# Decoded tokens' states and head norms as pieces of the streamed work of a hybrid decoder's mixers, and streamed work between dependent steps of VectorE

## The reference

```python
def _mixer(x, st, p, l):
    u = x @ p['w_in'][l] + p['b_in'][l]        # one projection for all branches and gates
    o_a, ... = _rwkv7(rw, ...)                  # RW: generalized delta rule, head norm
    o_b, ... = _mlstm(mqk, mv, mo, mi, mf, ...) # ML: matrix memory, causal conv, head norm
    o_c, ... = _gla(gq, gk, gv, gg, ga, ...)    # GL: gated linear attention, head rms
    o_d, ... = _rglru(rx, ry, ...)              # RG: gates, causal conv, linear scan
    up = einsum('blgc,gcd->blgd', branches, p['w_branch'][l])
    gate = sigmoid(gates.reshape(B, L, 4, 1024))
    return einsum('blgd,blgd->bld', gate, up) @ p['w_out'][l], new_states
```

## Time and profile before

| | us |
|---|---|
| median of 3 runs | 1965.49 |
| lowest, highest | 1957.01, 1965.77 |
| the profiled execution | 1960.32 |
| its span | 1958.5 |
| PE busy | 1805.5 (92%) |
| DVE busy | 1383.6 (71%) |
| ACT busy | 939.5 (48%) |

### The profile page before, as it was taken

The page is one execution under the profiler, slowest core; times in us unless marked ns, Lnnn a source line. Parts: engine busy times, 40 slices in busy tenths (PEclk is TensorE's granted clock), DMA queues, the critical chain, the costliest instruction groups (busy, mean ns, idle before and its releaser), DMA issues.

```text
span 1958.5 us, 26391 instructions
## 1 busy us (share of the span) xinstructions
PE 1805.5 (92%) x10174; PEld 1527.9 (78%) x10174; DVE 1383.6 (71%) x1619; ACT 939.5 (48%) x968; POOL 15.2 (1%) x32
## 2 busy tenths in 40 slices
PE   8799989979998989989986999999899999999896
PEld 7678878879997868868865877777687877777685
DVE  4857864445652758885425988989797979888794
ACT  4323422243332524422214666666576657766673
POOL 1000000000001000000000000000000000000000
PEclk9789999999998979999995999999999999999999
DMA  6233322334552324321223988989798978989770
GB/s 244 94 107 141 123 87 72 124 151 173 186 182 77 130 87 159 127 97 65 109 105 155 343 320 298 346 305 340 272 347 306 340 282 323 346 320 344 278 299 23
DMA packets 59307, 402.81 MB, mean 206 GB/s; under 512 B 8672, under 2 KB 9344, under 8 KB 11312
## 3 DMA queue, kind: packets, MB, share of 16 engines
q1 hardware_dynamic: 54144, 393.73, 54.0%
q0 software_dynamic: 1600, 3.97, 0.6%
q10 hardware_dynamic: 3440, 3.41, 0.5%
HBM read 396.60 MB, written 4.49 MB: 205 GB/s over the span
## 4 chain that ended last, share of the span: by engine, by line
PE 81%; DVE 11%; ACT 4%; issue 3%; DMA 0%; ACTq 0%; DVEq 0%; SPq 0%
PE mA L1906 48%; PE mW L1906 31%; ACT WH L703 2%; DVE slots_rounded L1270 1%; PE mA L1837 1%; DVE SCR L1235 1%; ACT X L994 1%; DVE SCR L1352 0%; DMA slots<-in_w_in_dram 0%; DVE V L1709 0%; DVE SCR L1347 0%; PE mW L1909 0%; DVE BIG L1285 0%; DVE HEL L1172 0%; DVE SCR L1237 0%
## 5 line engine op out<-in xcount | busy, mean ns | idle before, releaser
L1050 DVE TENSOR_TENSOR ring_low<-ring,WH 128x2048 fp32r<-128x2048 f32 x216 | 493.0, 2289 | 92.6 <-ACT WH L703 92.0
L703 ACT ACTIVATE WH<-ring 128x2048 fp32r<-128x2048 f32 x212 | 405.0, 1913 | 79.6 <-PE mW L1906 64.4
L1906 PE MATMUL mA<-XH,slots_rounded 128*128 128x264 f32 x1696 | 378.3, 297 | 10.2 <-DVE slots_rounded L1270 9.2
L1906 PE MATMUL mA<-WH,XEH 128*128 128x512 f32 x704 | 293.9, 418 | 8.2 <-DVE XEL L1140 6.9
L1906 PEld LDWEIGHTS mA<-XH,slots_rounded 128*128 128x128 f32 x1696 | 286.5, 194 | 17.8 <-issue 12.7
L1906 PE MATMUL mA<-WH,XEL 128*128 128x512 f32 x704 | 277.0, 393 | 0.0
L1906 PE MATMUL mA<-ring_low,XEH 128*128 128x512 f32 x608 | 240.2, 395 | 0.0
L1906 PE MATMUL mA<-XL,slots_rounded 128*128 128x264 f32 x672 | 197.2, 293 | 6.5 <-DVE small L1549 5.6
L1906 PEld LDWEIGHTS mA<-WH,XEH 128*128 128x128 f32 x704 | 133.1, 189 | 39.3 <-DVE ring_low L1050 10.6
L1906 PEld LDWEIGHTS mA<-WH,XEL 128*128 128x128 f32 x704 | 132.9, 189 | 31.9
L1906 PEld LDWEIGHTS mA<-XL,slots_rounded 128*128 128x128 f32 x672 | 130.3, 194 | 11.4 <-DVE small L1549 7.3
(11 more groups left out here) (396 smaller groups left out, 3135.7 us busy)
## 6 DMA issues: line engine op xcount, KB each, us to landing
ring<-in_moe_dram SPq DMA_DIRECT2D x216, 1024.0 KB, 4.8
slots<-in_w_in_dram SPq DMA_DIRECT2D x58, 1024.0 KB, 4.8
more_ring<-in_moe_dram SPq DMA_DIRECT2D x48, 1024.0 KB, 4.8
slots<-in_ffn_up_dram SPq DMA_DIRECT2D x22, 1024.0 KB, 4.8
slots<-in_ffn_down_dram SPq DMA_DIRECT2D x12, 1024.0 KB, 4.8
slots<-in_w_branch_dram SPq DMA_DIRECT2D x8, 1024.0 KB, 4.7
slots<-in_w_out_dram SPq DMA_DIRECT2D x8, 1024.0 KB, 4.8
con<-in_const_dram SPq DMA_DIRECT2D x1, 1441.0 KB, 14.4
```

Source lines behind the costliest of these rows:

```text
L703: nact.activation(WH[:, HI_SLOT[j % PAIR], :], expert_slot(j), ACT.Copy).then_inc(weights_hi, 1)
L1050: v.tensor_tensor(expert_low(j), expert_slot(j), WH[:, HI_SLOT[j % PAIR], :].bitcast(F32), SUB)\
L1906: return nc.tensor.matmul(out, w, x, start=start, stop=stop, skip_group_check=True)
```

## The change

It does five things in both mixers.

1. The decoded tokens' steps of ML, GL and RW and the head norms n1 and n2 leave the chain and become items of `STREAM`, of a new kind "tail", placed behind certain gate pairs. On TensorE they go through the `mA` banks in the stream's order; on VectorE and ScalarE they are yielded by the streamed work, in parts, the "rest" of a part behind the splits of the next pair. Their counters have new names (`mt.` for ML, `gt.` for GL, `rd.` for RW), and dependent steps among them have a semaphore of their own.
2. `link()` calls `fill("link1")`, `fill("link2")`, ... between a step's signal and its wait, so that streamed work can stand between dependent steps of VectorE.
3. The up tiles come earlier or later behind the gates (`BEHIND`).
4. The three tables have new numbers throughout; two lines of them stand in the diff. The heaviest numbers of TensorE's are now `"rg1": 450` (a point inside RG, ahead of `ml.qk`), `"rw.turned": 118`, `"rg.conv": 114` and `"rw.ops": 91`.
5. The states have semaphores of their own, and POOL's three waits are fewer: ML's state is loaded when `rg.conv` is done, GL's when `ml.cout` is, RW's when `rw.ops` is. Areas of memory move to make this possible, and VectorE gets three small copies (`MQK`, `DKN`, `DK4`) and loses one.

```diff
+TAILS = {(RG, 0): "ml.dvb", (RG, 1): "ml.dnum", (RG, 2): "ml.mean", (RG, 3): "ml.var", (ML, 0): "gl.dvb", (ML, 1): "gl.dy", (ML, 2): "gl.var", (GL, 2): "rw.dsa", (GL, 3): "rw.dy"}
+BEHIND = {RG: 1, ML: 1, GL: 1, RW: 4}
...
-PE_FILL = {"loads9": 25, "rg.conv": 95, "ml.qk": 228, "ml.logd0": 16, "ml.kw3": 9, "ml.abs": 7, "ml.h": 44,
+PE_FILL = {"loads9": 24, "rg.conv": 114, "rg1": 450, "ml.gcol": 14, "ml.kw3": 7, "ml.abs": 1, "ml.h": 52,
...
             def link(ins):
                 linked[0] += 1
+                links[0] += 1
+                own = linked[0]
                 ins.then_inc(dve_link, 1)
-                dve.wait_ge(dve_link, linked[0])
+                between[0](f"link{links[0]}")
+                dve.wait_ge(dve_link, own)
...
+                if name == "rw":
+                    dve.wait_ge(*dve_of.at("rw.ops", l))
+                    yield from linked_up(v.tensor_tensor(DY, unit(), over_v(vv[:, :, TP:T]), MUL))
+                    dve.wait_ge(rw_state_in, 16 * (l + 1))
+                    yield from named(v.tensor_tensor(DX, DS, over_v(DKN), MUL), "rd.dx")
+                    yield from linked_up(v.tensor_tensor(DS, DS, over_v(DW), MUL))
...
+                        while behind:
+                            yield from tail_of(behind.pop(0) + " rest")
+                        if TAILS.get(item[1:]) in ("ml.dvb", "gl.dvb", "rw.dsa"):
+                            yield from tail_of(TAILS[item[1:]][0:2])
...
+                    if name == "rw.dsa":
+                        pe.wait_ge(*dve_of.at("rd.dx", l))
+                        for k in range(4):
+                            ins = mm(into(k), bo, flat(DX if k < 2 else DY, k % 2))
...
-                pe.wait_ge(*dve_of.at("ml.dv", l))
-                for j in range(2):
-                    ins = mm(mW[:, j, :], bo, MX[:, j, :, :].rearrange("p b v -> p (b v)"))
-                ins.then_inc(*pe_of.step("ml.dvb"))
...
-                pool.wait_ge(*dve_of.at("gl.out", l))
-                pool.wait_ge(state_out, 16 * (12 * l + 9))
-                pool.dma_start(DS, A["rS"][l]).then_inc(layer_in, 16)
+                pool.wait_ge(*dve_of.at("rw.ops", l))
+                pool.dma_start(DS, A["rS"][l]).then_inc(rw_state_in, 16)
```

More of the change, by code:

```diff
@@ L47, with gate_behind @@
 FT = FF // P
+TAILS = {(RG, 0): "ml.dvb", (RG, 1): "ml.dnum", (RG, 2): "ml.mean", (RG, 3): "ml.var", (ML, 0): "gl.dvb", (ML, 1): "gl.dy", (ML, 2): "gl.var", (GL, 2): "rw.dsa", (GL, 3): "rw.dy"}
+BEHIND = {RG: 1, ML: 1, GL: 1, RW: 4}
 def streamed_work():
     seq = [("u", i) for i in (TMI - 1, TRX, TRY, TMQ, TMK, TMV, TMO, TGQ, TGV, TGG, TR, TK, TV)]
[L55 to L62, removed]
+    gates = [(g, q) for g in (RG, ML, GL, RW) for q in range(4)]
+    ups = list(gates)
+    for n, (g, q) in enumerate(gates):
+        seq.append(("gate", g, q))
+        while ups[0][0] != RW and gates.index(ups[0]) + BEHIND[ups[0][0]] <= n:
+            seq.append(("up",) + ups.pop(0))
+        if (g, q) in TAILS:
+            seq.append(("tail", TAILS[g, q]))
+    return seq + [("up",) + up for up in ups]
+def gate_behind(tail):
+    at, = (gate for gate, name in TAILS.items() if name == tail)
+    gates = [(g, q) for g in (RG, ML, GL, RW) for q in range(4)]
+    return gates[gates.index(at) + 1]
 STREAM = streamed_work()
-PAIRS = [item for item in STREAM if item[0] != "up"]
+PAIRS = [item for item in STREAM if item[0] in ("u", "gate")]
 PLAIN = 2
@@ L439, in program @@
         MCO = ar(2, 64)
+        MDT = ar(2, 4 * TD)
+        MQK = ar(4, TD)
         assert ar.at <= 12416, ar.at
@@ L665, in program @@
                         tiles += 1
+                if item[0] == "tail":
+                    for k, emptied_by in enumerate(TAIL_TILES[item[1]]):
+                        number(item[1], l, k, dve_of.at(emptied_by, l))
                 for _ in range(2):
@@ L841, in streamed @@
                             yield
+                            if q == 0 and item[0] == "gate":
+                                yield from tail(item[1:])
                 fill = filler(streamed(), ACT_FILL)
@@ L1260, in streamed @@
             def streamed():
-                l, up, n = layer[0], 0, 0
+                l, up, n, behind = layer[0], 0, 0, []
                 for item in STREAM:
+                    if item[0] == "tail":
+                        behind.append(item[1])
+                        continue
                     if item[0] != "up":
                         n += 1
-                        if PLAIN <= n < len(PAIRS):
+                        for name in behind:
+                            yield from tail_of(name)
+                        if n < len(PAIRS) and n >= PLAIN:
@@ L1977, in streamed @@
                             continue
+                        if item[0] == "tail":
+                            yield from tail_of(item[1])
+                            continue
                         _, g, q2 = item
```

469 lines of the change are left out of this document (275 added, 194 removed), and 13 rows, old and new, of tables (DVE_FILL, PE_FILL).

## The result

The changed kernel took 1909.93 us (median; 1907.43 to 1915.04), the kernel before, beside it on the same chip, 1961.49. The ratio is 0.974, 95% interval 0.970 to 0.978. In a second measurement it took 1905.83, ratio 0.972 (0.970 to 0.974).

What follows compares the result with a forecast made beforehand. TensorE was taken to wait for VectorE, mostly for late splits of streamed weights, and to lose time at half clock. Waits 9.4 us less plus clock 12.8 give 22.2; from 1960.3 that is 1938, put at 1942, range 1914 to 1965.

Steps and rivals of the forecast that it cites:

- I take 17: TensorE's waits between `ml.h` and `rw.ops` grow from 8.5 to 17 us a layer, between 4 and 22.
- The middle: Stretch from `ml.h` to `rw.ops`: VectorE's work, 61.5 us, would exceed TensorE's, 57.4, so TensorE waits at least 4.
- three places: VectorE held in the middle at GL's prompt result, ScalarE's late square roots, and the sums of GL's decoded tokens.
- Rival 2: The middle fits: VectorE's idle time is used up, waits stay near 8 us a layer; 1924 us, chance 0.12.
- Rival 1: ML's heads run at full clock because the gaps ahead are short: 16 us more gain, 1926 us, chance 0.14.
- Ahead of ML: Splits moved into the decays' chain and RG, 240 more streamed matmuls before `ml.qk`: waits 10.45 become 1.0 us a layer.
- `ml.gcol` and `rw.turned`: Waits at these two points fall from 1.6 to 0.2 and from 3.35 to 0 us a layer.
- RW's small steps: The states' small steps lose streamed tiles between them: waits 0.95 become 2.0 us a layer, between 1 and 5.
- The price of a place between steps: A split between two dependent VectorE steps gives back about 0.13 us, some 30 times a layer, a third counting: 2.6 us.
- The clock: TensorE's half clock falls from 88.5 us by 28.5, at 0.45 us each: 12.8 us gained; 30 a layer stay.
- Rival 3: The waits move, into the middle and `ml.qk`, and nothing is gained: 1958 to 1968 us, chance 0.19.
- Rival 4: The middle falls to half clock as TensorE stops every few us: slower, 1984 us, chance 0.09.

Runs made afterwards that it cites:

- two reciprocal experiments: Changed kernel with the reciprocal in ML's head norm replaced by an addition, 1913.74 us; and with that reciprocal taken twice, 1916.60 us.
- before_split_early: Kernel before with eight splits moved forward, four into the decays' chain, two behind it, two into ML's convolution: 1964.82 us, ratio 1.0017.
- before_tables_alone: Kernel before with early splits and 120 more streamed matmuls ahead of `ml.qk`, decoded steps still in the chain: 1974.52 us, ratio 1.006.
- tiles_between_heads: Changed kernel with 36 streamed matmuls, 12 each between ML's four heads, taken from ahead of `ml.h`: 1909.86 us, ratio 0.974.
- no_pause_and_tiles: Changed kernel with 462 instead of 450 streamed matmuls ahead of ML's heads and 12 each between them: 1916.64 us, ratio 0.977.
- heads_with_tiles: Changed kernel with 36 streamed matmuls taken from ahead of ML's heads (450 becomes 414) and put, 12 each, between them: 1923.73 us, ratio 0.980.

## Why the prediction was wrong in size

The direction was right, and most of the steps. The failed step is "I take 17": the middle's waits, with 4 and 22 as bounds.

- **The middle, failed.** The sums of work held: VectorE 60.8 us (61.5 forecast), PE 58.2 and 59.8 (57.4). The idle time of VectorE did not. The 17 are the 4.1 us by which VectorE's work was to exceed PE's and 12.9 of VectorE's idle time, which I put at three places; that idle time was 66.71 - 60.78 = 5.9, of which 4.37 at one of the three, the prompt's result of GL:

```profile
162.52 0.69 DVE L1672 COPY V<-mW 128x512 f32<-128x512 f32 x1 [4.37 <-PE mW L2022]
```

  At the square roots VectorE waits 0.42 us, because the norm's steps stand among RW's, and GL's sums found it busy. So PE waits 9.1 and 7.5: 17.4 us of the error over two layers, more than half of it. Rival 2 had the size (near 8 a layer); its condition, VectorE's idle time used up, was not met, since 6 us of it stay. Rivals 1 and 2 at once would give 1908, near the measured time, but neither came as described, so that nearness is luck. The two reciprocal experiments show that this idle time is no reserve: most of it lies ahead of the place where VectorE and ScalarE are both just in time.
- **Ahead of ML, right in size, wrong in its reason.** 10.45 us became 1.35 and 1.15 (1.0 forecast), PE arrives at 96.4 (97 forecast), and VectorE's operand is ready at 97.8 (96.2). But the splits' place in the decays' chain makes no difference, and earlier splits alone bring the wait to `ml.qk`. What is left, as far as these runs show, are the 240 matmuls, which stood in the working as a consequence, together with the tails, whose leaving the chain sets them free.
- **`ml.gcol` and `rw.turned`**: no wait left, as forecast within 0.2 us. **RW's small steps**: 0.6 us, at `rw.bk`, where 2.0 stood for the states, 2.8 us of the error over two layers.
- **The price of a place between steps.** The 2.6 us in all were too little, and although the prediction has them in its sum, none of its terms holds them: without the places 10 to 16 us are lost, with them behind the wait 16 to 20, an estimated half of that by the clock.
- **The clock.** 61.3 us at half clock were found (60 forecast), the heads more than half of them, 10.2 at most in the middle of a layer. PE's busy time fell by 17.2 us where 12.8 stood. The price of 0.45 from the earlier trace rows is near the 0.40 of the heads. By it the 27.2 us less of half clock (88.5 to 61.3) are worth 12.2; where the other 5 us of PE's busy time went no run shows.
- **Rival 1**, the heads at full clock: did not come with the change, though the pause ahead of them fell to 1.35 and 1.15 us. **Rival 3**, the waits move: that is before_split_early and before_tables_alone, not the change. **Rival 4**: the middle stopped every few us, and had only 6.8 and 10.2 us at half clock.

The sizes add up: the waits that went are 21.8 us more than forecast, the clock's gain is 4.4 more, and the changed kernel's median lies 2.3 below its profiled execution where I added 3.9. Together that is 32.4 us, for 1942 - 1909.9.

## What to carry to other kernels

Two streams on one in-order engine are worth separating by what each needs: steps that are only late results can go into the filler, and the filler that they no longer need as cover can be spent where a long operand is being made. Forecast the waits of a stretch from the order of its rows, place by place, and take the idle time of the other engine as large only where a row names what it waits for. Where two engines end together, test both directions: taking 3 us from one gained nothing, adding 3.45 cost some 4 us of waits a layer.

## What the runs showed of the hardware that was not expected

- The granted clock fell to 1.2 GHz (half) at ML's heads without a pause nearby: in the changed kernel at 105.49, 4 us into the heads and 7.7 us behind the last wait, of 1.35 us. With twelve 128x264 matmuls between each two heads and a wait of 1.15 us left ahead of them (`tiles_between_heads`), the half clock there was 3.4 and 6.8 us, where the changed kernel's two profiles have stretches of 13.7 to 27.3. But with the same matmuls between the heads and no wait at `ml.qk`, but one of 1.8 us behind it (`no_pause_and_tiles`), layer 0 had 3.4 and 10.2 us. What decides it the runs do not show. In a pause of 5.5 us it fell too, 2.7 us into it in layer 0 and 4.4 in layer 1 (`heads_with_tiles`). The Trainium skill ("TensorE: Matmul & The Clock Gate", section on why this matters) ties the fall to idle gaps between bursts; the 5.5 us pause agrees with it, and the changed kernel, where the fall comes 7.7 us behind a wait of 1.35 us, does not.
- The half clock cost 0.40 us for each us at the heads, not the 0.50 that it would if all of PE's time there doubled. What did not double no run shows.
- The order of one wait and one independent piece of work on VectorE, at 29 places a layer, moved the time by 16 to 20 us.
